# Row tiles turned to feature layout by transposing DMAs on ScalarE's queue instead of TensorE, with two bank pairs for the scores

## The reference

```python
z = x @ w_in                                       # 1024 -> 2560: u | v | gate_b | gate_c | x_in
u, v, gb, gc, xin = split(z)
v = layernorm(v)                                   # per head of 128
a = u * (masked w_s @ v + b_s)                     # mixes the 128 positions of a block
b = gb * causal_conv3(gc * xin)
x = layernorm(ALPHA * x + concat(a, b) @ w_out)    # sublayer 1
q = x @ w_q
p = softmax(q @ mem_k * 256 ** -0.5)               # 4 heads, 256 memory tokens
x = layernorm(ALPHA * x + (p @ mem_v) @ w_mem_o)   # sublayer 2
f = (silu(x @ w_gate) * (x @ w_up)) @ w_down       # 2816 wide
x = layernorm(ALPHA * x + f)                       # sublayer 3
```

## Time and profile before

| | |
|---|---|
| three runs, median | 3474.18 us (3464.06 to 3486.86) |
| the profiled execution | 3471.73 us, span of its slowest core (2) 3470.2 us |
| the eight cores' spans | 3429.2 to 3470.2 us |
| PE busy | 3272.9 us, 94% |
| DVE, ACT, POOL busy | 56%, 26%, 10% |
| mean granted TensorE clock | 0.972 to 0.984 |

### The profile page before, as it was taken

One profiled execution on the slowest core, in us unless ns is written; L12 is line 12 of the kernel. 1 busy time (PEld: TensorE's weight loads), 2 busy tenths in 40 slices (PEclk: granted clock), 3 DMA queues, 4 the chain that ended last, 5 costly groups with the idle time before them and its releaser, 6 DMA issues.

```text
span 3470.2 us, 49386 instructions; the slowest of 8 cores (3429.2 to 3470.2 us)
## 1 busy us (share of the span) xinstructions
PE 3272.9 (94%) x16482; PEld 1538.2 (44%) x16808; DVE 1949.7 (56%) x3428; ACT 899.7 (26%) x1687; POOL 333.0 (10%) x355
## 2 busy tenths in 40 slices
PE   5787999997999999999999999999999999999998
PEld 2433444443444444445344444444444444444443
DVE  4454554654656567565465656656564755656553
ACT  1421323222232231322223223231322223132320
POOL 1111101110001010010000101000010101000000
PEclk8789999998999999999999999999999999999997
DMA  9799899469474535445345453545445453544442
GB/s 165 134 218 199 169 233 219 165 193 213 174 184 173 192 122 208 153 178 199 109 169 186 152 197 138 204 147 207 151 152 205 141 215 138 194 163 164 183 146 79
DMA packets 95751, 601.52 MB, mean 173 GB/s; under 512 B 10992, under 2 KB 13168, under 8 KB 35408
## 3 DMA queue, kind: packets, MB, share of 16 engines
q1 hardware_dynamic: 82272, 507.17, 40.3%
q0 software_dynamic: 11808, 87.17, 15.7%
q10 hardware_dynamic: 1424, 4.02, 0.5%
HBM read 620.58 MB, written 71.18 MB: 199 GB/s over the span
## 4 chain that ended last, share of the span: by engine, by line
PE 76%; DMA 8%; DVE 7%; issue 4%; ACT 4%; another core or an unknown queue 1%; POOL 0%; DVEq 0%; SPq 0%; ACTq 0%; POOLq 0%
PE bank L332 74%; DMA ringA<-wpk 2%; DVE st L567 2%; PE bank L530 2%; DVE mv L569 1%; DMA ringB<-wsc 1%; ACT F L583 1%; ACT Pf L690 1%; DMA xbuf<-x_prompt 1%; DMA wsc<-ringA 1%; DMA fsc<-xbuf 1%; DMA wsc<-ringB 1%; DVE xbuf L803 1%; DVE nmx L687 1%
## 5 line engine op out<-in xcount | busy, mean ns | idle before, releaser
L332 PE MATMUL bank<-feat,ringB 128*128 128x512 bf16 x5516 | 1255.7, 382 | 14.3 <-DMA ringB<-wpk 4.9
L332 PEld LDWEIGHTS bank<-feat,ringB 128*128 128x128 bf16 x5632 | 552.6, 98 | 681.3 <-issue 47.1
L332 PE MATMUL bank<-ringB,hT 128*128 128x512 bf16 x2627 | 609.9, 382 | 33.4 <-DMA ringB<-wpk 23.8
L778 DVE TENSOR_TENSOR hT<-bank,scr 128x512 bf16<-128x512 f32 x352 | 238.2, 690 | 506.0 <-PE bank L332 291.1
L332 PE MATMUL bank<-ringA,F 128*128 128x512 bf16 x1927 | 449.5, 384 | 24.2 <-DMA ringA<-wpk 16.0
L332 PE MATMUL bank<-feat,ringA 128*128 128x512 bf16 x1995 | 457.2, 383 | 4.3 <-DMA ringA<-wpk 1.7
L500 POOL TENSOR_TENSOR rs<-ve,mhalf 128x1 f32<-128x1 f32 (+1 forms) x195 | 219.7, 1127 | 2463.2 <-DVE ve L498 2443.4
L332 PEld LDWEIGHTS bank<-ringB,hT 128*128 128x128 bf16 x2696 | 260.3, 98 | 341.1 <-issue 50.6
L523 ACT ACTIVATE row<-xbuf 128x1024 bf16<-128x1024 f32 x128 | 135.3, 1057 | 1043.4 <-DVE xbuf L513 1043.4
L332 PE MATMUL bank<-ringA,feat 128*128 128x512 bf16 x1449 | 336.2, 383 | 41.1 <-DMA ringA<-wpk 16.8
L332 PEld LDWEIGHTS bank<-feat,ringA 128*128 128x128 bf16 x2048 | 198.9, 99 | 234.2 <-issue 18.8
(11 more groups left out here) (118 smaller groups left out, 1852.5 us busy)
## 6 DMA issues: line engine op xcount, KB each, us to landing
ringB<-wsc SPq DMA_DIRECT2D x205, 1024.0 KB, 6.3
ringA<-wsc SPq DMA_DIRECT2D x103, 1024.0 KB, 6.9
ringA<-fsc SPq DMA_DIRECT2D x62, 1024.0 KB, 10.7
ringB<-wpk POOLq DMA_DIRECT2D x34, 1024.0 KB, 15.7
xbuf<-x_prompt SPq DMA_DIRECT2D x64, 512.0 KB, 8.9
y_prompt<-xbuf SPq DMA_DIRECT2D x64, 512.0 KB, 2.9
ringA<-wpk POOLq DMA_DIRECT2D x22, 1024.0 KB, 19.3
ringB<-wsc SPq DMA_DIRECT2D x25, 768.0 KB, 5.8
```

Source lines behind the costliest of these rows:

```text
L332: op("tensor", lambda e: e.matmul(out, lhsT=lhsT, rhs=rhs, start=start, stop=stop), reads=reads, writes=writes)
L778: op("vector", lambda e: e.tensor_tensor(out=hT[:, f, :], in0=bu, in1=sg[:, 0:512], op=ALU.mult), reads=[bbu, bsg], writes=[b_hT[f]])
```

## The change

`to_feat` becomes one transposing DMA of a whole `row` tile (128x1024 bf16, or 64x1024) straight into `feat` or `F1`, issued from ACT's queue, each sub on a semaphore of its own. It takes no PSUM bank, no matmul and no ACT copy. `ident` and its two POOL instructions go. `ln_full` calls `x_to_feat` itself, so the transposing DMA stands on ACT right behind the copy to `row`; all later `x_to_feat` calls are dropped. The `p_to_feat` calls stay where they were. With no transposes on PE during the scores, `zone` is banks 4 to 7 and `pairs` is (4, 6) there; in tile 7, where bank 7 is held by the sample rows, it stays at one pair.

```diff
-        ident = T("ident", [128, 128], BF16)
...
@@ ln_full and to_feat
             op("scalar", lambda e, r=s.row: e.activation(out=r[0:SP, :], in_=s.x[0:SP], func=AF.Copy), reads=[s.bx], writes=[s.brow])
-
-
-        def to_feat(src, b_src, SP, dst, b_dst):
-            bk, bb = take()
-            bv = bk.bitcast(BF16)
-            for c in range(8):
-                op("tensor", lambda e, c=c: e.transpose(bv[:, c * SP:(c + 1) * SP], src[0:SP, c * 128:(c + 1) * 128], ident[0:SP, 0:SP]),
-                   reads=[b_src, buf("ident")], writes=[bb])
-            op("scalar", lambda e: e.activation(out=dst, in_=bv[:, 0:8 * SP].rearrange("p (c t) -> p c t", c=8), func=AF.Copy),
-               reads=[bb], writes=b_dst)
-            give(bb)
+            x_to_feat(s)
+
+
+        def to_feat(src, b_src, SP, dst, b_dst, stream):
+            op("scalar", lambda e: e.dma_start(out=dst, in_=src[0:SP, :], transpose=True), reads=[b_src], writes=b_dst, dma=stream)
 
         def x_to_feat(s):
-            to_feat(s.row, s.brow, s.SP, s.F0, [s.bF0])
+            to_feat(s.row, s.brow, s.SP, s.F0, [s.bF0], "tx%d" % s.j)
...
@@ the tile loop: every x_to_feat call goes, as here
             pc = use_piece("in_v")
-            x_to_feat(prev[2])
             in_v(subs[0], pc)
-            x_to_feat(prev[3])
             in_v(subs[1], pc)
...
             d = down_half(prev, 0)
-            zone[0], pairs[0] = (6,) if smp_f else (6, 7), (4,)
+            zone[0], pairs[0] = ((6,), (4,)) if smp_f else (range(4, 8), (4, 6))
             pc = [use_piece("qk0"), use_piece("qk1")]
             scores(subs[0], pc)
-            x_to_feat(subs[3])
```

More of the change, by code:

```diff
@@ L364, in sample_sub @@
             return s
[L367 to L370, removed]
         op("gpsimd", lambda e: e.memset(mhalf[:], -0.5), writes=[buf("mhalf")])
@@ L710, in p_to_feat @@
         def p_to_feat(s):
-            to_feat(s.row, s.brow, s.SP, s.F1, s.bF1)
+            to_feat(s.row, s.brow, s.SP, s.F1, s.bF1, "tp%d" % s.j)
         def sample_q(s):
@@ L934, in build @@
             proj_resid(subs[j], pc, subs[j].F1, subs[j].bF1, 0)
-            if j > 1:
-                x_to_feat(subs[j - 2])
         mem_proj("mk", mk_o, 0)
-        x_to_feat(subs[2])
         mem_proj("mk", mk_o, 1)
-        x_to_feat(subs[3])
         load_ln(1)
@@ L1013, in build @@
             pc = use_piece("in_v")
-            x_to_feat(prev[2])
             in_v(subs[0], pc)
-            x_to_feat(prev[3])
             in_v(subs[1], pc)
-            if smp_f:
-                x_to_feat(prev[4])
             v_stats(subs[0])
@@ L1053, in build @@
                 f(2)
-                if j:
-                    x_to_feat(subs[j - 1])
             if smp:
@@ L1064, in build @@
             d = down_half(prev, 0)
-            zone[0], pairs[0] = (6,) if smp_f else (6, 7), (4,)
+            zone[0], pairs[0] = ((6,), (4,)) if smp_f else (range(4, 8), (4, 6))
             pc = [use_piece("qk0"), use_piece("qk1")]
             scores(subs[0], pc)
-            x_to_feat(subs[3])
-            if smp:
-                x_to_feat(ss)
             d(5)
@@ L1093, in build @@
             d(6)
-            x_to_feat(subs[0])
             proj_resid(subs[2], pc, subs[2].F1, subs[2].bF1, 1)
             d(5)
-            x_to_feat(subs[1])
             if smp:
```

## The result

The change makes the kernel slower: median 3790.9 us (3727.76 to 4024.7, 4 runs) against 3469.12 us (3454.52 to 3486.86, 4 runs) of the kernel before beside it. The profiled execution took 3750.2 us, its slowest core (7) 3748.6 us. The prediction was 3402 us, range 3365 to 3500: wrong in sign.

The account below looks back on a forecast made before the run. It took PE, busy 94% of the span, as the bound. Terms -54 - 1 - 17 - 9 - 3 + 2 + 10 + 2 = -70 us took the profiled 3471.7 to 3402 us, range 3365 to 3500.

Parts of the forecast that it names:

- The transposes: PE freed of transposes, 0.45 us a row tile: 54 us gained in tiles 4 to 15, about 1 for sample rows.
- The bank pairs: At the scores, waits on `hT` and `Pf` both go: 1.85 us a tile, 17 us in all.
- The rows without cover: Sub 3 after sublayer 2, read by a tile's first `gate_up`: loses T - 3.85 us, 0.15 a tile, 2 in twelve tiles.
- T: Time from the end of the copy to `row` until the transposed row tile has landed; taken as 4.0 us.
- the wait moves, and eats half: Rival: at each tile start T is 6.2 us, losing 2.35 plus about 1.4 for clock; 3445 us, chance 0.16.
- On ACT ... even an issue of some us hides: On ACT, the DMA issue replaces a copy and costs nothing, as ACT idles 148 of 203 us.
- Most row tiles have far more cover: Sublayer 1 rows and probabilities are needed behind other PE steps, so their landing was priced at no wait.
- That fits: In the DMA engines, a row tile takes 0.74 us, twelve 9 us a tile: share 0.52 for 0.48.
- a gain of 9 + 3 there: First tiles: 9 us gained in tiles 1 to 3, of a possible 19, and 3 of tile 0's 5.4.
- 10 for late landing: Starts of three first tiles: landing at 10.4 us loses 6.6 each; 10 of 20 us counted as lost.
- The turning itself is slow: Rival: T is 10.4 us, each tile's first `gate_up` loses 8 us; +37, 3509 us, chance 0.15.
- A denser PE loses clock: Rival: middle tiles without transposes run at clock 0.81, 47 us more each; three give 3543 us, chance 0.05.

Follow-up runs that it names:

- the pairs alone: Kernel before plus only the bank change (scores zone banks 4 to 7, pairs (4, 6)), TensorE still transposing: ratio 0.9956 to the kernel before.
- the kernel that turns 8 covered row tiles by DMA: Against the pairs alone: from tile 7, rows of sublayer 1 and probabilities turned by DMA where the transposes stood, TensorE turning the rest: 0.9971 to the kernel before.
- The kernels with `x1` by TensorE and by DMA: `x1` is `x` after sublayer 2. TensorE: DMA only for sublayer 1 rows and probabilities from tile 7 (0.9971; later `xT` load 0.9842). DMA: change, sublayer 1 late (1.0763).
- The aside copies in 2 KB pieces: The pairs alone plus a plain DMA copy of each row tile from ACT's queue, 2 KB pieces, into a side tile nobody reads: 1.0136 to the kernel before.
- the kernel with the later load: DMA for sublayer 1 rows and probabilities from tile 7, as in the 0.9971 kernel, plus the next tile's `xT` load issued after the last probabilities: 0.9842, 3416.25 us.
- x0 late: The change with only sublayer 1's turning DMAs moved to where the transposes stood, behind silu; those of sublayer 2 right behind the copy to `row`: 1.0763.
- plain 256-byte pieces: The change with each transposing DMA replaced by a plain copy, unturned, same place, queue and 256-byte pieces: 1.0326 to the kernel before.

## Why the prediction was wrong

**The transposes: right.** From the pairs alone to the kernel that turns 8 covered row tiles by DMA, a tile falls from 197.9 to 193.3 us: 4.6 us, 0.57 a row tile, where I had 0.45.

**The bank pairs: right in size.** 15 us for 17, though with TensorE transposing only the wait on `hT` went. With the change the one on `Pf` went, and the one on `hT` came back longer, because silu is late (below).

**The rows without cover: the mechanism right, the sizes low.** At the place that the prediction names, T was 5.7 us in the median for 4.0. The sum had no loss of clock there (only the rivals had one, 1.4 us from the earlier trace rows); it was 2.9. The kernels with `x1` by TensorE and by DMA differ by 197.7 - 193.4 = 4.3 us a tile, in the median of tiles 8 to 13 over the eight cores; with the 1.8 saved by four row tiles that is some 6 us lost, where the sum had 0.15. T and the clock give 5.7 - 3.85 + 2.9 = 4.8 of them. The rival "the wait moves, and eats half" had 3.75.

**"On ACT ... even an issue of some us hides": the step that failed in the middle tiles.** I had compared the issue with ACT's idle share. What counts is what stands behind it: silu, and behind silu DVE's product, the sums of the next sub and the bank of the first `scores`. An issue of 1.2 to 1.5 us in each of the four rounds, which had no slack, became some 5 us a tile (8.4 in the quiet ones of the slowest core). ACT was idle through most of it. The prediction named this only in its last list, without a price.

**"Most row tiles have far more cover" and "That fits": the steps that failed in the first tiles.** I took 0.74 us of all engines for a row tile, at the rate of the large pieces. The aside copies in 2 KB pieces cost 4.3% of 3493.9 us / 195 = 0.77, so that rate holds for plain large pieces; in 256-byte pieces it was 6.7% of 3573.6 / 195 = 1.2, turned 2.7. And I took the late landings of the first tiles as 10.4 us at three tile starts. At these starts core 7 had T of 19.6, 9.8 and 6.1 us, and PE waited 44.5 us for 20. But a row of sublayer 1 that I had as covered landed after 72.6 us, and 178 of the 239 us of waits on turned rows are outside the tile starts, with ACT held meanwhile. This is the larger loss, 49 + 184 of 278 us; the sum had a gain of 9 + 3 there and 10 for late landing. The weights' casts fill the engines there, but no experiment took them away; that they, and not another load of the first tiles, make the rows late is argued from the DMA rows of 890 to 940.

**The rivals.** "The turning itself is slow" had the right sign and the wrong place: its T of 10.4 us is met at no start of tiles 8 to 14 on any core (9.5 at the most), and what it missed is the hold on ACT. For a single row tile the median landing with the change was 7.1 us for `x` and 6.5 for the probabilities. "A denser PE loses clock" is out: the last window above is 99.6% dense at 1.00. The range ended at 3500 because every rival priced one wait per tile, and none a queue that backs up beside the casts.

The Trainium skill ("Advanced Engine Details and Errata", section "X-Bar Transpose (TRN2)") says that "TRN2 transpose DMAs are as fast as regular DMAs" and expects 350 to 400 GB/s. This case disagrees. Bytes over the time of all 16 engines give 103 GB/s as a mean over the run with the change (54.77 MB in 14.2% of 3748.6 us) and 156 GB/s in the quiet window of 200 us of the kernel with the later load (8 row tiles, 2.10 MB in 6.7%); the plain 2 KB pieces aside reach 364 (54.75 MB in 4.3% of 3493.9 us).

What stays open: why a turning packet sometimes takes six times as long beside POOL's DMAs, and whether the holds are the queue's limit or the engines'. A long hold comes with an earlier row tile still unfinished (176 of 177), but that is not enough for one (381 short ones had it too), and no experiment varied the number in flight alone.

## What to carry to other kernels

Work taken off the busiest engine is only worth its time if what takes its place is priced where it stands in the order of its own engine: ask what is queued right behind a DMA issue, not how idle the issuing engine is. Price a DMA by the size of its pieces, and look at what other queues move in the same microseconds; a turning DMA in 256-byte pieces goes well in quiet stretches with cover, and went badly beside POOL's loads. When a good change has a few bad tiles, look in these for what they share: moving one load took the ratio from 0.9971 to 0.9842.

## What the runs showed of the hardware

- The issue of a turning DMA of 128x1024 bf16 held ACT for 1.23 us at the least, that of a plain one in 256-byte pieces for 0.60, in 2 KB pieces for 0.47; the longest holds on the slowest core were 48.16 us with the change, 69.73 with x0 late, 41.25 with plain 256-byte pieces and 0.53 with 2 KB pieces.
- Landing of a turned row tile with the change was 3.1 us at the least, in the median 7.1 for `x` and 6.5 for probabilities, 72.6 at the most.
- After PE waits of 2.97 and 2.96 us the granted clock was 0.52 and 0.72 in the 6 us behind them; 16 matmuls took 6.50 and 5.30 us for 3.62.
